# Expert weight ring of eight blocks, two of them over buffers of the first mixer, and an expert loop of four experts per turn

## The chip, the cores and the metric

One core of one Trainium2 chip runs the whole program in one launch. The metric is the device time in microseconds (us) of one execution. The kernel before takes 1587.86 us, the median of 3 runs (1586.34 to 1592.57).

## The reference, cut to what matters

Two transformer blocks follow one another on one sequence of 256 tokens with 1024 features, all in float32. The change lies in the first block, at the seam between its mixer and its routed experts:

```
def first_block(x, ...):
    mix = token_mixer(x, ...)            # x @ w_in, sliding-window attention beside
                                         # gated spatial mixing, then @ w_out
    h   = layer_norm(2**0.25 * x + mix)
    ffn = routed_experts(h, ...)         # 32 experts, 4 per token, d_ff = 1024
    return layer_norm(2**0.25 * h + ffn)

def expert(xb):                          # xb: the rows routed to this expert
    gt  = minimum(xb @ w_gate + b_gate, 7)
    up  = clip(xb @ w_up + b_up, -7, 7)
    hid = gt * sigmoid(1.702 * gt) * (up + 1)
    return hid @ w_down + b_down         # then times the token's gate, added to its row
```

Each expert has three 1024 x 1024 float32 matrices, 12 MB; all 32 experts together have some 400 MB. The second block (RWKV-7 mixing, block attention, a gated feed-forward layer with a convolution) is not touched, apart from where some of its inputs lie.

## The kernel before, in words

**Memory.** There are two areas in SBUF. `ring` has 24576 floats per partition, `work` has 27500. During the experts `ring` is six slots of 4096 floats (`SLOTS = 6`, `SLOT = 4096`, 2 MB per block over 128 partitions). An expert is six blocks: blocks 0 to 3 hold two 128-row slices each of gate and up weights (`UP_SLOTS = 4`), blocks 4 and 5 hold four slices each of the down weights. Block j of every expert goes to slot j. Before the experts, `ring` holds `w_in` (slots 0 to 3) and `w_out` (slots 4 and 5) of the mixer. `work` holds everything else: constants, the broadcast bias and norm rows (`rows_sb`), the attention and gating tensors, x (`x_nat`), h.

**The order of the loads.** All large loads are issued by SyncE (SP) on one queue, in program order. For the first expert (L448 to L451) it waits until the projections are done (`proj_done` 6), issues slots 0 to 3, waits until the whole mixer product is done (`mix_done` 4), and issues slots 4 and 5. It then waits for `iter_ready` (the routing is known), issues seven small loads for the second block (L454 to L462), reads two loop counts, and enters its loop. A turn of the loop (L465 to L469) is one expert: for each of the six slots it waits until TensorE has used the slot's old block and issues the new one. After the loop it issues the weights of the second block in half buffers (L471 to L477); the first four halves go into the area of slots 0 and 1 and wait for the last expert to be through with these slots.

**The expert loop on the engines.** The number of turns is 32 as long as no expert has more than 64 rows. In one turn TensorE (PE) adds the biases (L669), multiplies the four up blocks (L692), gathers the rows of the next expert (L652), scatters the result of the expert before (L661), transposes (L705, L709), multiplies the two down blocks (L719). ScalarE and VectorE do the activation and the copies between these. Each matmul group waits for its slot by a count that rises by 16 per turn (`slot_in[j]`), and adds one to `slots_used`, by which SP refills. Every instruction of the turn stands once in the program and is run 32 times.

**Around it.** Before the loop PE does the mixer's output product (`project_out`, L603) in two halves: slices 0 to 3 of `w_out` for both token tiles, then slices 4 to 7. Then come the layer norm on VectorE, the router product (L631) and the counts (L640 to L644). GpSimd (POOL) computes the low-order parts of h (L2022, L2024, semaphore `rest_ready`).

Of the kernel before, what the change touches and what calls it, by code (L numbers as in the profile page):

```python
# [33 lines left out]
SLOTS = 6  # L34
UP_SLOTS = 4
SPLITS = 3
BIAS_ROWS = SPLITS * NE
# [6 lines left out]

ROWS = [("b_in_vug", W_VUG), ("ln_v_g", G1), ("ln_v_b", G1), ("b_router", NE), ("sinks", NQ),
        ("b_out", D), ("ln1_g", D), ("ln1_b", D), ("ln2_g", D), ("ln2_b", D)]
COLUMNS = [("b_in_qk", 5), ("b_s", NG)]
# [64 lines left out]
def program(nc, A, out):  # L112
    ctx = ExitStack()
    with ctx:
        def sem(name):
            return ctx.enter_context(nc.semaphore(name))
# [23 lines left out]
        cols_sb = take(cols_n)  # L140
        rows_sb = take(rows_n)
        const = lambda n: const_sb[:, const_at[n][0]:sum(const_at[n])]
# [10 lines left out]
        def little(*shape):  # L153
# [13 lines left out]
        ss1, rms1 = little(TT), little(TT)  # L167
        w_router = take(KD * NE).rearrange("p (k e) -> p k e", k=KD)
        n_iter = ctx.enter_context(nc.sbuf_tensor("n_iter", [1, 2], I32))

# [3 lines left out]
        w_out = ring[:, 16384:24576].rearrange("p (k n) -> p k n", k=KD)  # L174
        x_nat = take(TT * D).rearrange("p (t d) -> p t d", t=TT)
# [8 lines left out]
        prob = take(3 * 1024)  # L184
        prob0 = prob[:, 0:1024].rearrange("p (h s) -> p h s", h=NQ)
# [20 lines left out]
        place = pool2[:, 2560:2624].bitcast(BF16).rearrange("p (t s) -> p t s", t=TT)  # L206
        alpha_ident = take(P)
        bias_area = take(3 * D // 2)
        bias_parts = bias_area.bitcast(BF16)
# [15 lines left out]
            sem(n) for n in ("pT_done", "pT_ready", "attn_done", "attn_ready", "sguT_done", "sguT_ready"))  # L225
        mix_done, var_ready, std_ready, h_ready, hT_done, hT_ready = (
            sem(n) for n in ("mix_done", "var_ready", "std_ready", "h_ready", "hT_done", "hT_ready"))
# [3 lines left out]
        slot_in = [sem(f"slot_in{i}") for i in range(SLOTS)]  # L231
        slots_used = sem("slots_used")
# [183 lines left out]

        def slot_area(j):
            return ring[:, j * SLOT:(j + 1) * SLOT]

        def up_slot(j):  # L420

            return slot_area(j).rearrange("p (b k n) -> p b k n", b=2, k=2)

        def down_slot(j):
            return slot_area(UP_SLOTS + j).rearrange("p (k n) -> p k n", k=4)

        @block.sync
        def _(sp):
# [4 lines left out]
            sp.dma_start(cols_sb, A["columns"]).then_inc(consts_in, 16)  # L433
            mix_n = rows_at["b_out"][0]
            sp.dma_start(rows_sb[:, 0:mix_n], A["rows"][0:mix_n].partition_broadcast(P)).then_inc(consts_in, 16)

# [5 lines left out]
            sp.dma_start(x_nat, A["x"].rearrange("(t p) d -> p t d", p=P)).then_inc(ln_rows_in, 16)  # L442
            sp.dma_start(rows_sb[:, mix_n:rows_n], A["rows"][mix_n:rows_n].partition_broadcast(P)).then_inc(ln_rows_in, 16)
# [18 lines left out]
            sp.dma_start(rows2_sb, A["rows2"].partition_broadcast(P)).then_inc(small2_in, 16)  # L462
            n = sp.value_load(n_iter[0:1, 0:1], min_val=NE, max_val=NE * PASSES)
            n_rest = sp.value_load(n_iter[0:1, 1:2], min_val=NE - 1, max_val=NE * PASSES - 1)
            with sp.Fori(1, n) as it:  # L465
                e = it % NE
                for j in range(SLOTS):
                    sp.wait_ge(slots_used, sp.snap(it * SLOTS - (SLOTS - j - 1)))
                    sp.dma_start(slot_area(j), expert_slot(e, j)).then_inc(slot_in[j], 16)  # L469

            for n2, (f, half) in enumerate(HALVES):  # L471
                if n2 < 4:
                    sp.wait_ge(slots_used, sp.snap(n_rest * SLOTS + n2 * HBUF // SLOT + 1))
                else:
                    sp.wait_ge(half_used, n2 - 3)
                w = half_width(f)
                sp.dma_start(half_view(n2), A[f"w2_{f}"][:, half * w:(half + 1) * w]).then_inc(half_in[n2 % 4], 16)  # L477
# [35 lines left out]
        def _(pe):  # L513
# [86 lines left out]
            def project_out(t, ks):  # L600
                for n in range(2):
                    for k in ks:
                        ins = pe.matmul(bank[mix_bank[t][n]][:, :], mixT[:, k, t * P:(t + 1) * P], w_out[:, k, n * BANK:(n + 1) * BANK],  # L603
                                        start=k == 0, stop=k == KD - 1)
                    if ks[-1] == KD - 1:
                        ins.then_inc(mix_done, 1)

            pe.wait_ge(attn_ready, 2)
# [68 lines left out]
            pe.wait_ge(iter_ready, 1)  # L677
            n = pe.value_load(n_iter[0:1, 0:1], min_val=NE, max_val=NE * PASSES)
            with pe.Fori(0, n) as it:
                now, ahead, landed = pe.snap(it + 1), pe.snap(it + 2), pe.snap(it * 16 + 16)  # L680

# [31 lines left out]
                for j in range(SLOTS - UP_SLOTS):  # L713
                    pe.wait_ge(slot_in[UP_SLOTS + j], landed)
                    w = down_slot(j)
# [6 lines left out]
            pe.wait_ge(y_ready, pe.snap(n + 1))  # L722
            pe.wait_ge(place_T_ready, pe.snap(n + 1))
            scatter(True).then_inc(acc_done, 1)
# [420 lines left out]
        def _(act):  # L1145
# [61 lines left out]
            act.wait_ge(iter_ready, 1)  # L1207
            n = act.value_load(n_iter[0:1, 0:1], min_val=NE, max_val=NE * PASSES)
            with act.Fori(0, n) as it:
                now, ahead = act.snap(it + 1), act.snap(it + 2)  # L1210
                act.wait_ge(gt_ready, now)
# [4 lines left out]
                act.copy(hidT, bank[4][:, :].rearrange("p (j c) -> p j c", j=4)).then_inc(hidT_ready, 1)  # L1216
                act.wait_ge(slots_used, act.snap(it * SLOTS + SLOTS))
                act.copy(yy, bank[7][:, :]).then_inc(y_ready, 1)  # L1218

            for n2 in range(2):  # L1220
# [227 lines left out]
        def _(dve):  # L1448
# [177 lines left out]
            link(dve.tensor_reduce(n_iter_f[0:1, 0:1], bank[4][0:1, 0:NE], AX.X, ALU.max))  # L1626
            link(dve.tensor_scalar(passes, const("thresholds")[0:1, :], n_iter_f[0:1, 0:1], float(NE), ALU.is_lt, ALU.mult))
            link(dve.tensor_reduce(n_iter_f[0:1, 1:2], passes, AX.X, ALU.add))
# [19 lines left out]
            build_place(1)  # L1648
            n = dve.value_load(n_iter[0:1, 0:1], min_val=NE, max_val=NE * PASSES)
            with dve.Fori(0, n) as it:  # L1650
                now = dve.snap(it + 1)
                dve.wait_ge(slots_used, dve.snap(it * SLOTS + UP_SLOTS))
                dve.tensor_scalar(gt, bank[4][:, :], LIMIT, None, ALU.min).then_inc(gt_ready, 1)  # L1653
# [7 lines left out]
                dve.wait_ge(place_T_done, now)  # L1661
                pick(bass.ds((it + 1) % NE, 1))
                dve.tensor_copy(place_T, bank[5][:, 0:T]).then_inc(place_T_ready, 1)
                build_place(it + 2)
                build_place_g(it + 1)

# [442 lines left out]
```

## Time and profile before

| | |
|---|---|
| median of 3 runs | 1587.86 us (1586.34 to 1592.57) |
| the profiled execution | 1587.55 us, its span 1585.7 us |
| mean granted TensorE clock | 0.984 |
| PE busy | 1454.2 us (92%) |
| DMA, HBM read | 489.73 MB, mean 309 GB/s over the span |
| chain of waits: share of DMA of expert weights | 45% |
| chain of waits: share of PE | 46% |

The span is what lies between the first and the last instruction. The execution's own time is 1.85 us longer than its span. The page's strip of 40 slices has slices of 39.6 us: one digit is the busy share in tenths. The chain of waits follows the work that ended last back in time, so its shares tell which resource set the end, while busy shares do not.

### The profile page before, as it was taken

The page shows a single profiled execution, that of the slowest core. Times are in us where ns is not written, and L with a number is a line of the kernel's source. Part 1 is how long each engine was busy: PE and PEld are TensorE (multiplying, and loading weights), DVE is VectorE, ACT ScalarE, POOL GpSimd, SP SyncE. Part 2 cuts the span into 40 slices and gives each one's busy share as a digit, 9 for nine tenths or more (in the row PEclk, how much of TensorE's full clock was granted, in tenths as well). Part 3 has the DMA queues.
Part 4 walks back from the last instruction along what each step waited for, and adds up shares of the span by engine and source line. Part 5 has one row for each costly group of instructions (what it writes and reads, how often), then busy time and mean ns, then how long its engine had stood idle before and what let it go on. Part 6 is the DMA issues. An engine that isn't in the chain of part 4 may idle for free.

```text
span 1585.7 us, 22051 instructions
## 1 busy us (share of the span) xinstructions
PE 1454.2 (92%) x9246; PEld 806.3 (51%) x9246; DVE 515.2 (32%) x888; ACT 365.5 (23%) x507; POOL 70.7 (4%) x34
## 2 busy tenths in 40 slices
PE   8989998989989989989889889869998999999998
PEld 6543333323333333333333333339777895489997
DVE  1762211112112112111111111156794535266565
ACT  0531111101101101101111111135545220244542
POOL 0020000000000000000000000000000000023322
PEclk9999999999999999999999999989999989999999
DMA  9659999999999999999999999945440015135552
GB/s 366 222 227 367 429 428 429 428 428 429 428 428 428 429 429 429 429 427 429 429 429 428 428 428 429 429 187 171 148 139 21 2 54 235 45 136 185 188 193 80
DMA packets 44527, 491.24 MB, mean 310 GB/s; under 512 B 4944, under 2 KB 5456, under 8 KB 13168
## 3 DMA queue, kind: packets, MB, share of 16 engines
q1 hardware_dynamic: 44352, 490.66, 75.2%
q8 instruction: 24, 0.39, 0.1%
q10 hardware_dynamic: 144, 0.13, 0.0%
q14 instruction: 7, 0.06, 0.0%
HBM read 489.73 MB, written 1.05 MB: 309 GB/s over the span
## 4 chain that ended last, share of the span: by engine, by line
PE 46%; DMA 45%; DVE 5%; ACT 3%; issue 1%; SPq 0%; DVEq 0%; ACTq 0%
DMA ring<-in_w_exp 45%; PE bank L692 10%; PE bank L740 5%; PE bank L741 5%; PE bank L742 5%; PE bank L719 2%; PE bank L1065 2%; PE bank L603 2%; PE bank L1103 2%; PE bank L521 1%; PE bank L551 1%; DVE ring_parts L1684 1%; PE bank L661 1%; PE bank L652 1%; PE bank L908 0%
## 5 line engine op out<-in xcount | busy, mean ns | idle before, releaser
L692 PE MATMUL bank<-ring,work 128*64 128x512 f32 x2048 | 460.8, 596 | 67.8 <-DMA ring<-in_w_exp 67.8
L692 PEld LDWEIGHTS bank<-ring,work 128*64 128x64 f32 x2048 | 139.4, 136 | 371.4 <-issue 227.9
L1653 DVE TENSOR_SCALAR work<-bank 128x512 f32<-128x512 f32 x32 | 22.1, 692 | 721.9 <-PE bank L692 721.9
L719 PE MATMUL bank<-ring,work 128*64 128x512 f32 x1024 | 226.8, 595 | 14.6 <-ACT work L1216 14.6
L719 PEld LDWEIGHTS bank<-ring,work 128*64 128x64 f32 x1024 | 70.6, 137 | 150.2 <-issue 128.0
L740 PE MATMUL bank<-work_parts,ring_parts 128*128 128x256 f32 x472 | 132.8, 281 | 5.4 <-DVE work_parts L1702 5.4
L1212 ACT ACTIVATE work<-work 128x512 f32<-128x512 f32 x32 | 20.2, 631 | 500.3 <-DVE work L1653 500.3
L741 PE MATMUL bank<-work_parts,ring_parts 128*128 128x256 f32 x472 | 133.2, 282 | 0.0
L742 PE MATMUL bank<-work_parts,ring_parts 128*128 128x256 f32 x472 | 133.0, 282 | 0.0
L740 PEld LDWEIGHTS bank<-work_parts,ring_parts 128*128 128x128 f32 x472 | 91.1, 193 | 6.4 <-issue 5.7
L741 PEld LDWEIGHTS bank<-work_parts,ring_parts 128*128 128x128 f32 x472 | 90.6, 192 | 0.8
L742 PEld LDWEIGHTS bank<-work_parts,ring_parts 128*128 128x128 f32 x472 | 90.7, 192 | 0.0
L740 PE MATMUL bank<-ring_parts,work_parts 128*128 128x512 f32 x200 | 80.5, 402 | 3.2 <-DVE ring_parts L1684 2.5
L741 PE MATMUL bank<-ring_parts,work_parts 128*128 128x512 f32 x200 | 79.2, 396 | 0.0
L742 PE MATMUL bank<-ring_parts,work_parts 128*128 128x512 f32 x200 | 79.0, 395 | 0.0
L1401 ACT CAST ring_parts<-ring 128x2048 fp32r<-128x2048 f32 (+1 forms) x44 | 63.4, 1467 | 50.2 <-PE bank L742 50.2
L1218 ACT COPY work<-bank 128x512 f32<-128x512 f32 x32 | 18.8, 586 | 230.0 <-PE bank L719 230.0
L661 PE MATMUL bank<-work 64*128 64x512 f32 x264 | 65.6, 614 | 0.7 <-ACT work L1218 0.7
L2036 POOL TENSOR_TENSOR ring_parts<-ring,ring_parts 128x1024 fp32r<-128x1024 f32 x22 | 55.9, 2541 | 225.5 <-ACT ring_parts L1401 225.5
L652 PEld LDWEIGHTS bank<-work 128*128 128x128 bf16 x1584 | 49.9, 98 | 26.9 <-issue 26.9
L1980 DVE TENSOR_TENSOR ring_parts<-ring,ring_parts 128x2048 fp32r<-128x2048 f32 x21 | 54.1, 2575 | 21.0 <-ACT ring_parts L1401 21.0
L2030 POOL TENSOR_TENSOR ring<-ring,work 128x512 f32<-128x512 f32 x4 | 5.1, 1276 | 1168.1 <-DVE ring L1878 1168.1
(392 smaller groups left out, 1609.3 us busy)
## 6 DMA issues: line engine op xcount, KB each, us to landing
ring<-in_w_exp SPq DMA_DIRECT2D x192, 2048.0 KB, 24.1
ring<-in_ffn_up SPq DMA_DIRECT2D x22, 1024.0 KB, 4.8
ring<-in_ffn_down SPq DMA_DIRECT2D x22, 512.0 KB, 3.3
ring<-in_w_in SPq DMA_DIRECT2D x2, 2048.0 KB, 16.7
ring<-in_w_out SPq DMA_DIRECT2D x4, 1024.0 KB, 16.7
ring<-in_w_k SPq DMA_DIRECT2D x4, 1024.0 KB, 5.0
ring<-in_w_v SPq DMA_DIRECT2D x4, 1024.0 KB, 4.9
ring<-in_w_gate_a SPq DMA_DIRECT2D x4, 1024.0 KB, 4.9
```

The lines of the kernel that those rows point to most:

```text
L603: ins = pe.matmul(bank[mix_bank[t][n]][:, :], mixT[:, k, t * P:(t + 1) * P], w_out[:, k, n * BANK:(n + 1) * BANK], start=k == 0, stop=k == ...
L652: ins = pe.matmul(x_bank[:, k * CAP:(k + 1) * CAP], h_part[:, part, t, k * P:(k + 1) * P], place[:, t, :], start=n == 0, stop=n == 5, skip ...
L661: ins = pe.matmul(bank[2 * t + n][:, :], place_T[lo:lo + CAP, t * P:(t + 1) * P], yy[lo:lo + CAP, :], start=False, stop=stop, skip_group_c ...
L692: ins = pe.matmul(to[n2 * CAP:(n2 + 1) * CAP, :], x_e[:, 2 * j + kk, :], w[:, b, kk, n2 * BANK:(n2 + 1) * BANK], start=False, stop=j == UP ...
L719: ins = pe.matmul(y_bank[n2 * CAP:(n2 + 1) * CAP, :], hidT[:, k % 4, k // 4 * CAP:(k // 4 + 1) * CAP], w[:, kk, n2 * BANK:(n2 + 1) * BANK] ...
L740: pe.matmul(to, left[0], right[0], start=start, stop=False, skip_group_check=True)
L741: pe.matmul(to, left[0], right[1], start=False, stop=False, skip_group_check=True)
L742: return pe.matmul(to, left[1], right[0], start=False, stop=stop, skip_group_check=True)
L1065: ins = pe.matmul(bank[to[n2] + t][:, :], yT[:, k, t * P:(t + 1) * P], tail[f][:, k, n2 * BANK:(n2 + 1) * BANK], start=k == 0, stop=k == N ...
L1401: act.copy(ff_hi[i][:, cols], ff_land[i][:, cols]).then_inc(ff_upper[i], 1)
L1980: dve.tensor_tensor(ff_rest[i][:, 0:2 * D], ff_land[i][:, 0:2 * D], ff_hi[i][:, 0:2 * D].bitcast(F32), ALU.subtract).then_inc(up_rest[i], 1)
L2036: pool.tensor_tensor(ff_rest[i][:, 2 * D:FF], ff_land[i][:, 2 * D:FF], ff_hi[i][:, 2 * D:FF].bitcast(F32), ALU.subtract).then_inc(down_res ...
```

## The change: what it does

- The ring gets eight slots (`RING = 8`). Slots 6 and 7 lie in `work`. Slot 6 lies over the end of `rows_sb`, over `wsT`, `qkT` and `v_nat`; slot 7 lies over `ug` (which also holds h) and `x_nat`. For this the rows, `prob`, `x_nat`, `alpha_ident` and `bias_area` get other places; the sizes and numbers of their loads stay.
- Blocks go round the ring: block number n of the whole stream goes to slot n mod 8. As 24 blocks are four experts and three rounds, the loop's turn on every engine becomes four experts (`TURN = 4`), written out, and there are 8 turns for 32 experts.
- Before the loop SP issues eight blocks, in the order 0, 1, 2, 3, 6, 4, 5, 7. Block 6 (expert 1, block 0) waits for the gating product and the last biases. Block 4 waits for a new semaphore after the first half of the mixer's output product (`mix_first`). Block 5 waits for `mix_done` 4, as before. Block 7 waits for `rest_ready` 4 and `router_done` 2.
- SP's loop runs one turn less than the others, with 24 refills per turn (blocks 8 to 31 counted from the turn's first block); the last 16 refills stand behind it. The half buffers wait for the blocks that last lie in slots 0 and 1.

```diff
+RING = 8
+TURN = 4
+PER_TURN = TURN * SLOTS // RING
@@
+        prob = take(3 * 1024)
+        seventh_at = top[0] - 3 * 1024 - SLOT
+        eighth_at = top[0]
         ug = take(2 * TT * G1)
+        x_nat = take(TT * D).rearrange("p (t d) -> p t d", t=TT)
@@
-        def slot_area(j):
-            return ring[:, j * SLOT:(j + 1) * SLOT]
+        def slot_area(s):
+            return ring[:, s * SLOT:(s + 1) * SLOT] if s < SLOTS else work[:, (seventh_at, eighth_at)[s - SLOTS]:][:, 0:SLOT]
+        def slot_of(turn, j):
+            return (turn * SLOTS + j) % RING
+        def landed_count(it, turn, j):
+            return (it * PER_TURN + (turn * SLOTS + j) // RING + 1) * 16
@@ SP
-            for j in range(SLOTS):
-                if j == UP_SLOTS:
-                    sp.wait_ge(mix_done, 4)
-                sp.dma_start(slot_area(j), expert_slot(0, j)).then_inc(slot_in[j], 16)
+            for s in (0, 1, 2, 3, 6, 4, 5, 7):
+                if s == 6:
+                    sp.wait_ge(mixed_done, 1)
+                    sp.wait_ge(ug_biased, 4)
+                if s == 4:
+                    sp.wait_ge(mix_first, 1)
+                if s == 5:
+                    sp.wait_ge(mix_done, 4)
+                if s == 7:
+                    sp.wait_ge(rest_ready, 4)
+                    sp.wait_ge(router_done, 2)
+                sp.dma_start(slot_area(s), expert_slot(s // SLOTS, s % SLOTS)).then_inc(slot_in[s], 16)
@@ SP
-            with sp.Fori(1, n) as it:
-                e = it % NE
-                for j in range(SLOTS):
-                    sp.wait_ge(slots_used, sp.snap(it * SLOTS - (SLOTS - j - 1)))
-                    sp.dma_start(slot_area(j), expert_slot(e, j)).then_inc(slot_in[j], 16)
+            def refill(it, load):
+                s = load % RING
+                e = (it * TURN + load // SLOTS) % NE
+                sp.wait_ge(slots_used, sp.snap(it * (TURN * SLOTS) + (load - RING + 1)))
+                sp.dma_start(slot_area(s), expert_slot(e, load % SLOTS)).then_inc(slot_in[s], 16)
+            with sp.Fori(0, n_rest) as it:
+                for load in range(RING, RING + TURN * SLOTS):
+                    refill(it, load)
+            for load in range(RING, TURN * SLOTS):
+                refill(n_rest, load)
@@ half buffers
-                    sp.wait_ge(slots_used, sp.snap(n_rest * SLOTS + n2 * HBUF // SLOT + 1))
+                    sp.wait_ge(slots_used, sp.snap(n_rest * (TURN * SLOTS) + (TURN * SLOTS - RING + 1 + n2 * HBUF // SLOT)))
@@ PE
-            project_out(1, range(0, 4))
+            project_out(1, range(0, 4)).then_inc(mix_first, 1)
@@ PE, ACT and DVE alike: the body of the loop becomes expert(it, turn)
-                    pe.wait_ge(slot_in[j], landed)
-                    w = up_slot(j)
+                    s = slot_of(turn, j)
+                    pe.wait_ge(slot_in[s], pe.snap(landed_count(it, turn, j)))
+                    w = up_slot(s)
...
+            with pe.Fori(0, n) as it:
+                for turn in range(TURN):
+                    expert(it, turn)
@@ DVE
-            link(dve.tensor_scalar(passes, ..., float(NE), ALU.is_lt, ALU.mult))
+            link(dve.tensor_scalar(passes, ..., float(NE // TURN), ALU.is_lt, ALU.mult))
```

## Rows read from the trace of the kernel before

**Rows 1.** The page: the instruction queue, then the chain's shares by engine.

```profile
q8 instruction: 24, 0.39, 0.1%
...
PE 46%; DMA 45%; DVE 5%; ACT 3%; issue 1%; SPq 0%; DVEq 0%; ACTq 0%
```

**Rows 2.** The chain that ended last: start us, length us, what.

```profile
149.51 13.73 PE bank L692 x64
...
175.82 13.73 PE bank L692 x64
...
216.04 23.44 DMA ring<-in_w_exp
...
243.35 25.50 DMA ring<-in_w_exp
...
272.72 25.50 DMA ring<-in_w_exp
```

**Rows 3.** Stretches: busy us (count) per engine, clock, DMA share, GB/s.

```profile
43.00:49.00 6.00, 6.00 (x25) 3.32 (x24) 4.65 (x7) 5.20 (x23) 0.00 (x0) 1.00 0.96 410
...
93.00:101.00 8.00, 8.00 (x22) 3.61 (x21) 5.84 (x9) 0.29 (x1) 0.00 (x0) 1.00 0.00 1
...
113.00:120.00 7.00, 4.31 (x28) 2.07 (x27) 5.85 (x23) 3.00 (x6) 2.84 (x2) 0.74 0.00 0
122.00:127.00 5.00, 5.00 (x25) 1.74 (x26) 2.34 (x10) 1.87 (x2) 0.00 (x0) 0.88 0.79 252
...
400.00:1000.00 600.00, 540.04 (x3338) 197.14 (x3334) 80.67 (x200) 75.30 (x102) 0.00 (x0) 1.00 1.01 428
```

**Rows 4.** Timeline of SP: its first small load and its first refill.

```profile
120.16 0.33 SPq L454 DMA_DIRECT2D work<-in_consts  x1
...
127.16 0.36 SPq L469 DMA_DIRECT2D ring<-in_w_exp  x1
```

**Rows 5.** Timelines of POOL and PE: what ends rest_ready and router_done 2.

```profile
114.86 2.14 POOL L2024 TENSOR_TENSOR work<-work 128x1024 bf16<-128x1024 f32 x1 [1.16 <-ACT work L1188]
...
118.07 0.39 PE L642 MATMUL bank<-work 128*128 128x32 f32 x2
```

**Rows 6.** Blocks 0 to 3 (L451), few issues per window: issue, landing.

```profile
L451 SPq DMA_DIRECT2D ring<-in_w_exp x1: 347/347/347, 69.2 to 69.2; - x1
...
DMA to landing us min/median/max: 7.6/7.6/7.6
...
L451 SPq DMA_DIRECT2D ring<-in_w_exp x2: 432/432/432, 69.6 to 70.0; - x2
...
DMA to landing us min/median/max: 12.1/14.3/16.5
...
L451 SPq DMA_DIRECT2D ring<-in_w_exp x1: 534/534/534, 70.5 to 70.5; - x1
...
DMA to landing us min/median/max: 22.5/22.5/22.5
```

**Rows 7.** DMA queues, 86 to 93 us: packets, MB, share of 16 engines.

```profile
q8 instruction: 1, 0.02, 1.0%
```

**Rows 8.** The same, 139 to 150 us, then 150 to 1060 us (no q8).

```profile
q8 instruction: 1, 0.02, 0.5%
...
q1 hardware_dynamic: 26751, 384.79, 99.4%
```

**Rows 9.** L469: landing of the refill issued at 127.2, and the one at 137.1.

```profile
DMA to landing us min/median/max: 9.5/9.5/9.5
...
L469 SPq DMA_DIRECT2D ring<-in_w_exp x1: 333/333/333, 137.1 to 137.1; - x1
...
DMA to landing us min/median/max: 14.3/14.3/14.3
```

**Rows 10.** Second block, 1073 to 1089 us, and the queues of 1073 to 1090.

```profile
1073.00:1089.00 16.00, 16.00 (x139) 16.00 (x139) 11.21 (x20) 7.61 (x8) 0.00 (x0) 1.00 0.58 198
...
q8 instruction: 2, 0.03, 0.8%
```

More of the change, by code:

```diff
@@ L43 @@
 W_QK, W_QKV, W_VUG = 640, 768, 1152
-ROWS = [("b_in_vug", W_VUG), ("ln_v_g", G1), ("ln_v_b", G1), ("b_router", NE), ("sinks", NQ),
-        ("b_out", D), ("ln1_g", D), ("ln1_b", D), ("ln2_g", D), ("ln2_b", D)]
+ROWS = [("b_out", D), ("ln1_g", D), ("ln1_b", D), ("ln2_g", D), ("ln2_b", D),
+        ("b_router", NE), ("sinks", NQ), ("b_in_vug", W_VUG), ("ln_v_g", G1), ("ln_v_b", G1)]
 COLUMNS = [("b_in_qk", 5), ("b_s", NG)]
@@ L140, in program @@
         cols_sb = take(cols_n)
-        rows_sb = take(rows_n)
         const = lambda n: const_sb[:, const_at[n][0]:sum(const_at[n])]
@@ L168, in program @@
         w_router = take(KD * NE).rearrange("p (k e) -> p k e", k=KD)
+        alpha_ident = take(P)
+        bias_area = take(3 * D // 2)
+        rows_sb = take(rows_n)
         n_iter = ctx.enter_context(nc.sbuf_tensor("n_iter", [1, 2], I32))
@@ L174, in program @@
         w_out = ring[:, 16384:24576].rearrange("p (k n) -> p k n", k=KD)
-        x_nat = take(TT * D).rearrange("p (t d) -> p t d", t=TT)
         r2_at = top[0]
@@ L225, in program @@
             sem(n) for n in ("pT_done", "pT_ready", "attn_done", "attn_ready", "sguT_done", "sguT_ready"))
-        mix_done, var_ready, std_ready, h_ready, hT_done, hT_ready = (
-            sem(n) for n in ("mix_done", "var_ready", "std_ready", "h_ready", "hT_done", "hT_ready"))
+        mix_first, mix_done, var_ready, std_ready, h_ready, hT_done, hT_ready = (
+            sem(n) for n in ("mix_first", "mix_done", "var_ready", "std_ready", "h_ready", "hT_done", "hT_ready"))
         router_done, top_ready, top_exp, chosen_ready = (
@@ L230, in program @@
         iter_ready, split_ready = sem("iter_ready"), sem("split_ready")
-        slot_in = [sem(f"slot_in{i}") for i in range(SLOTS)]
+        slot_in = [sem(f"slot_in{i}") for i in range(RING)]
         slots_used = sem("slots_used")
@@ L415, in expert_slot, with up_slot, down_slot @@
             return A["w_exp"][bass.ds(e, 1), j, :, :].rearrange("o p n -> p (o n)")
-        def slot_area(j):
-            return ring[:, j * SLOT:(j + 1) * SLOT]
[L420 to L425, printed above, removed]
+        def slot_area(s):
[4 more added lines that the diff above has]
+            return (it * PER_TURN + (turn * SLOTS + j) // RING + 1) * 16
+        def up_slot(s):
+            return slot_area(s).rearrange("p (b k n) -> p b k n", b=2, k=2)
+        def down_slot(s):
+            return slot_area(s).rearrange("p (k n) -> p k n", k=4)
         @block.sync
@@ L433, in _ @@
             sp.dma_start(cols_sb, A["columns"]).then_inc(consts_in, 16)
-            mix_n = rows_at["b_out"][0]
-            sp.dma_start(rows_sb[:, 0:mix_n], A["rows"][0:mix_n].partition_broadcast(P)).then_inc(consts_in, 16)
+            mix_at = rows_at["b_router"][0]
+            sp.dma_start(rows_sb[:, mix_at:rows_n], A["rows"][mix_at:rows_n].partition_broadcast(P)).then_inc(consts_in, 16)
             sp.dma_start(w_in[:, :, W_QKV + G1:], A["w_in"][:, :, W_QKV + G1:]).then_inc(w_g_in, 16)
@@ L442, in _ @@
             sp.dma_start(x_nat, A["x"].rearrange("(t p) d -> p t d", p=P)).then_inc(ln_rows_in, 16)
-            sp.dma_start(rows_sb[:, mix_n:rows_n], A["rows"][mix_n:rows_n].partition_broadcast(P)).then_inc(ln_rows_in, 16)
+            sp.dma_start(rows_sb[:, 0:mix_at], A["rows"][0:mix_at].partition_broadcast(P)).then_inc(ln_rows_in, 16)
             sp.wait_ge(attn_done, 1)
@@ L606, in project_out @@
                         ins.then_inc(mix_done, 1)
+                return ins
             pe.wait_ge(attn_ready, 2)
@@ L677, in _, with expert @@
             pe.wait_ge(iter_ready, 1)
-            n = pe.value_load(n_iter[0:1, 0:1], min_val=NE, max_val=NE * PASSES)
-            with pe.Fori(0, n) as it:
-                now, ahead, landed = pe.snap(it + 1), pe.snap(it + 2), pe.snap(it * 16 + 16)
+            n = pe.value_load(n_iter[0:1, 0:1], min_val=NE // TURN, max_val=NE * PASSES // TURN)
+            def expert(it, turn):
+                now, ahead = pe.snap(it * TURN + (turn + 1)), pe.snap(it * TURN + (turn + 2))
                 pe.wait_ge(place_T_ready, now)
@@ L713, in _ @@
                 for j in range(SLOTS - UP_SLOTS):
-                    pe.wait_ge(slot_in[UP_SLOTS + j], landed)
-                    w = down_slot(j)
+                    s = slot_of(turn, UP_SLOTS + j)
+                    pe.wait_ge(slot_in[s], pe.snap(landed_count(it, turn, UP_SLOTS + j)))
+                    w = down_slot(s)
                     for kk in range(4):
@@ L1207, in _, with expert @@
             act.wait_ge(iter_ready, 1)
-            n = act.value_load(n_iter[0:1, 0:1], min_val=NE, max_val=NE * PASSES)
-            with act.Fori(0, n) as it:
-                now, ahead = act.snap(it + 1), act.snap(it + 2)
+            n = act.value_load(n_iter[0:1, 0:1], min_val=NE // TURN, max_val=NE * PASSES // TURN)
+            def expert(it, turn):
+                now, ahead = act.snap(it * TURN + (turn + 1)), act.snap(it * TURN + (turn + 2))
                 act.wait_ge(gt_ready, now)
@@ L1216, in _ @@
                 act.copy(hidT, bank[4][:, :].rearrange("p (j c) -> p j c", j=4)).then_inc(hidT_ready, 1)
-                act.wait_ge(slots_used, act.snap(it * SLOTS + SLOTS))
+                act.wait_ge(slots_used, act.snap(it * (TURN * SLOTS) + (turn + 1) * SLOTS))
                 act.copy(yy, bank[7][:, :]).then_inc(y_ready, 1)
+            with act.Fori(0, n) as it:
+                for turn in range(TURN):
+                    expert(it, turn)
             for n2 in range(2):
@@ L1648, in _, with expert @@
             build_place(1)
[L1649 to L1652, printed above, removed]
+            n = dve.value_load(n_iter[0:1, 0:1], min_val=NE // TURN, max_val=NE * PASSES // TURN)
+            def expert(it, turn):
+                now = dve.snap(it * TURN + (turn + 1))
+                dve.wait_ge(slots_used, dve.snap(it * (TURN * SLOTS) + (turn * SLOTS + UP_SLOTS)))
                 dve.tensor_scalar(gt, bank[4][:, :], LIMIT, None, ALU.min).then_inc(gt_ready, 1)
@@ L1661, in _ @@
                 dve.wait_ge(place_T_done, now)
-                pick(bass.ds((it + 1) % NE, 1))
+                pick(bass.ds((it * TURN + (turn + 1)) % NE, 1))
                 dve.tensor_copy(place_T, bank[5][:, 0:T]).then_inc(place_T_ready, 1)
-                build_place(it + 2)
-                build_place_g(it + 1)
+                build_place(it * TURN + (turn + 2))
+                build_place_g(it * TURN + (turn + 1))
+            with dve.Fori(0, n) as it:
+                for turn in range(TURN):
+                    expert(it, turn)
             def norm(t, rms):
```

12 lines of the change are left out of this document (4 added, 8 removed).

## The prediction

> **What bounds the kernel now.** I read the chain of waits first. DMA and PE share it almost evenly [rows 1], and in order of time it changes hands once in the expert loop. The first experts follow one another at PE's own pace, 175.82 - 149.51 = 26.31 us each. From 216.04 each expert ends on a transfer of weights, and the period is 272.72 - 243.35 = 29.37 us [rows 2]. The stretches say why: from 400 to 1000 us the DMA engines are fully busy at 428 GB/s [rows 3]. An expert is six blocks, so a block takes 29.37 / 6 = 4.895 us of all DMA engines. The loop is a stream of blocks at that pace. PE has 3.06 us to spare per expert. A deeper ring cannot make a saturated stream faster. It can only let the stream start earlier, in time in which the DMA engines now stand still. The stretches show such time: 93 to 101 us (share 0.00), 113 to 120 us (0.00), and some of 122 to 127 us (0.79) [rows 3].
>
> **Part 1, two blocks out of the loop.** Block 6 waits for things that are over before block 3 is in, and follows block 3 on the queue. Blocks 6 and 4 then fill 93 to 101 us. Block 5 goes out when it does now. Block 7 waits for POOL, which ends at 114.86 + 2.14 = 117.00, and for PE's L642, which ends at 118.46 [rows 5]. So it goes out near 118.5 us. The refills then have 184 blocks to bring instead of 186: -2 x 4.895 = -9.8 us.
>
> **Part 2, block 7 in front of the small loads.** The seven small loads go out from 120.16 us, as now, and the first refill at 127.16 [rows 4]. Block 7 is 118.5 to 120.16 = 1.7 us ahead of them and holds the engines for 4.9 us, so they are pushed back by 3.2 us. The idle fifth of 122 to 127 us can take up 0.21 x 5 = 1.05 us of it. So the refills begin 2.2 to 3.2 us later than now. I take the middle: +2.7 us. The small loads themselves are needed only after the loop.
>
> **Part 3, instruction fetches of PE inside the stream.** The profile has a queue q8 of kind instruction: 24 packets, 0.39 MB, so 16 KB each [rows 1]. Their size against the program points to PE. In the second block two of them lie in one dense stretch of 139 matmuls and 139 weight loads [rows 10], so a fetch brings about 260 to 280 instructions. PE runs 3338 matmuls and as many weight loads in 600 us of loop [rows 3], that is 163 of each per expert, 327 instructions. A turn of one expert is 1.2 fetches long. A turn of four is 1308 instructions and some for registers, 4.8 to 5.1 fetches. Now one fetch falls into the first turn (139 to 150 us), and none into 150 to 1060 us: the turn stays in the engine's memory [rows 8]. With four experts per turn I count four more fetches in the first turn, all in the saturated stream.
>
> What does one cost? Blocks 0, 1, 2 landed at 76.8, 81.7 and 86.5 us, 4.9 us apart. Block 3 landed at 70.5 + 22.5 = 93.0, 6.5 us behind block 2 [rows 6]. In that stretch one fetch ran [rows 7]. A block is in when the slowest of the 16 DMA engines has its share in. I read the 1.6 us as one engine held up by the fetch. A saturated stream never gives this back: the others are full too, but the landing waits for the late one. If all fetches of PE use the same engine, four of them add 4 x 1.6 = 6.4 us to it.
>
> That engine has some slack. The fetch at 139 to 150 us moved no landing: the refills of 127.2 and 137.1 landed at 136.7 and 151.4, three blocks in 14.7 us, 4.9 each [rows 9]. The first refill took 9.5 us to land against 7.6 alone [rows 6, 9], so some engine was 1.9 us behind the rest then, from uneven small loads. The fetch's engine was not that one: it had 1.9 us of room and used 1.6. With four more it ends 6.4 - 0.3 = 6.1 us behind where the slowest is now.
>
> This is the number between far ends. Below, it is 0: four fetches on four engines, each within the 1.9 us of room. Above, it is a fetch of every page in every turn (a rival below). I take 6.1, because the one fetch that hit a full stream with no slack moved a landing.
>
> **Edits at nothing.** The register arithmetic for each slot and turn on PE, ACT and DVE is hidden by PE's 3.06 us to spare per expert; it would have to exceed that to show, and costs up to some tenths in the last expert. SP waits for `slots_used` between refills and has several blocks queued. SP has no new wait in the loop; in front of it stand the waits of blocks 6 and 4, with block 5 behind them, all over before 101 us, and that of block 7, over before `iter_ready`. The half buffers stay behind the last block on the queue. Transfers into `work` run as fast as into `ring`: 43 to 49 us, with rows and x going to `work`, shows 410 GB/s at share 0.96, 427 per full share, against 428 [rows 3]. The bound from 410 would be 4% on a quarter of the blocks, 9 us; I take 0. The lead of eight blocks makes PE run at its own pace some three experts longer, and changes no end.
>
> **The sum.** -9.8 + 2.7 + 6.1 = -1.0 us. The profiled execution took 1587.55 us with a span of 1585.7, 0.31 under the median, so the difference carries over to the median: 1587.86 - 1.0 = 1586.9 us. All work behind the loop moves with its end. Changes under 0.5% (7.9 us) can't be told from none in this kernel.
>
> **Rival 1, the fetches cost nothing visible** (other engines, or a fetch that takes only its share). The sum is -9.8 + 2.7 = -7.1: 1580.8 us. For it: the fetch of 139 to 150 us moved no landing. Against it: block 3. If the idle parts also take all of block 7, it is -9.8: 1578.1 us, the most that this change can give.
>
> **Rival 2, slower: PE's turn no longer stays in its memory.** A turn of about five fetches is run eight times. If less than six pages are kept, each turn fetches them all again: 8 x 5.5 = 44 fetches instead of one, each on a full stream. That is 44 x 1.6 - 1.9 = 68.5 us more, and with parts 1 and 2 1587.86 - 7.1 + 68.5 = 1649 us. PE's own stall at each jump back hides in its 4 x 3.06 us per turn; the price is in the late DMA engine. For it: nothing here has a turn longer than 1.3 fetches. Against it: no fetch was made again when the turn crossed a page at each pass [rows 8]. It decides from the number of pages kept.
> The Trainium skill states this rule, in "Runtime: NRT & Kernel Launch", section "Instruction fetch mechanics": a taken branch to a target outside the current two-page window forces a fetch of the target page. By it the time is that of rival 2. The same section gives PE room for 128 KiB, by which the turn fits and nothing is fetched twice. The trace sides against a window of two: the fetch of the page ahead did not push out the loop's first page.
>
> **Rival 3, the blocks in `work` are slower, or the added instructions delay the end:** up to +9 us on -1.0, 1596 us. Only the 410 speaks for it.
>
> **How the numbers follow.** My forecast 0.45, rival 1 0.28 (of which 0.05 near the full 9.8), rival 2 0.17, rival 3 0.10. The range reaches from the full gain (1578.5) to somewhat short of rival 3 (1594) and leaves out rival 2 and a little at each end. Faster by over 0.5% needs under 1579.9: the best part of rival 1 and a share of its spread, 0.14. Slower by over 0.5% needs over 1595.8: rival 2 and half of rival 3, 0.22. The rest, 0.64, is no change that can be told.
>
> **What would show it.** Right: stretches 93 to 101 and 118 to 124 us busy on DMA; the first transfer that ends an expert two to three experts later than 216 us; a period of still 29.37 us at the end; q8 with some four more packets, all before 250 us; single landings of the first turn 6.5 us behind the one before instead of 4.9. Rival 1: the same q8 count and landings 4.9 us apart throughout, the loop's end 7 us earlier. Rival 2: q8 with over 60 packets, a mean period over 31 us. I am wrong altogether if the period changes without more fetches, or if the part behind the loop changes its length by more than 1 us.

## The result and the profile after

The changed kernel takes 1577.55 us (median of 5 runs, 1576.71 to 1578.58) against 1587.87 us (5 runs of before, 1586.34 to 1596.17). The ratio is 0.9922, with a 95% interval of 0.9895 to 0.9949. Its profiled execution took 1577.55 us with a span of 1575.6. A second set of runs, shown below, gave 1578.7 us and 0.9934 (0.9912 to 0.9955). The forecast was 1586.9 us, within 1578.5 to 1594.0: the time lies under the range, and the kernel is faster by 9 to 10 us where 1 us was forecast.

The page after. The columns are those of [rows 1] and [rows 3].

```profile
span 1575.6 us, 21819 instructions
...
DMA  9579999999999999999999999945440015145552
...
q8 instruction: 28, 0.46, 0.1%
...
PE 61%; DMA 29%; DVE 5%; ACT 3%; issue 1%; SPq 0%; DVEq 0%; ACTq 0%
```

q8 has four more packets than in [rows 1]. The DMA share of the chain fell from 45% to 29% without the stream getting any faster. In the full stream the chain now has one piece of DMA per two experts, 35.30 of 58.74 us, where it had 25.50 of each 29.37 us [rows 2]. Both chains belong to a stream of the same pace, so the shares of the chain say little on how much one resource bounds.

The chain in order of time (start us, length us, what):

```profile
150.78 13.74 PE bank L725 x64
...
177.10 13.74 PE bank L725 x64
...
256.11 13.74 PE bank L725 x64
...
289.47 30.77 DMA ring<-in_w_exp
...
343.70 35.28 DMA ring<-in_w_exp
...
402.45 35.30 DMA ring<-in_w_exp
...
461.19 35.30 DMA ring<-in_w_exp
...
1025.11 3.65 PE bank L725 x16
```

PE's own pace is the same (26.32 us per expert). The first transfer in the chain starts at 289 us, where it was 216 us in [rows 2]. From then on two experts take 461.19 - 402.45 = 58.74 us, 29.37 each, as before. The last line is PE's work on the last up block of the last expert, for which it waited at the end of the stream. Before, the same group starts 7.3 us later:

```profile
1032.40 3.65 PE bank L692 x16
```

The stretches after (busy us and counts, clock, DMA share, GB/s):

```profile
93.00:101.00 8.00, 8.00 (x20) 3.50 (x19) 5.84 (x9) 0.29 (x1) 0.00 (x0) 1.00 0.94 398
103.00:111.00 8.00, 4.84 (x28) 3.33 (x29) 7.74 (x9) 3.62 (x7) 5.20 (x2) 0.96 0.57 233
113.00:118.00 5.00, 4.75 (x12) 2.58 (x11) 3.10 (x10) 2.33 (x2) 3.17 (x2) 0.58 0.00 0
...
122.00:127.00 5.00, 5.00 (x46) 2.58 (x45) 3.47 (x14) 1.87 (x2) 0.00 (x0) 0.80 0.90 381
400.00:1000.00 600.00, 538.38 (x3346) 197.34 (x3343) 81.22 (x201) 54.15 (x85) 0.00 (x0) 1.00 1.01 429
```

The idle time of [rows 3] between 93 and 101 us is filled by blocks 6 and 4. The stretch from 122 to 127 us went from 0.79 to 0.90. 113 to 118 us is still empty. The stream itself has the same 429 GB/s.

SP's timeline, to be read against [rows 4]: block 7 goes out 1.62 us ahead of the small loads. The fence behind it is the summary of the DMA of the first refill, which takes 9.6 us to land.

```profile
119.80 0.33 SPq L473 DMA_DIRECT2D work<-in_w_exp  x1
121.42 0.33 SPq L476 DMA_DIRECT2D work<-in_consts  x1
...
126.26 1.20 SPq L484 DMA_DIRECT2D work<-in_rows  x1
```

```profile
DMA to landing us min/median/max: 9.6/9.6/9.6
```

q8 by stretch, the answer to [rows 8]: one fetch from 139 to 150 us, and four from 150 to 1060 us, where there were none.

```profile
q8 instruction: 1, 0.02, 0.6%
...
q1 hardware_dynamic: 26546, 381.73, 98.6%
q8 instruction: 4, 0.07, 0.0%
```

The difference between the two first profiles splits into two parts. The start of the last x16 group moved by 1032.40 - 1025.11 = 7.3 us. From that group to the end of the span there are 1585.7 - 1032.40 = 553.3 us before and 1575.6 - 1025.11 = 550.5 after, 2.8 us less. Together 10.1. The first part is the size of rival 1 (7.1 us). The second was in no forecast. The experiments ask for both.

### The profile page after: what moved, and what is told of

Read it like the earlier page. It is cut to its first block, busy times and chain, and to the rows that moved or that the text cites. A ratio compares the mean times of both kernels' runs of the same rounds, so it can differ in the third digit from the quotient of the medians.

```text
span 1575.6 us, 21819 instructions
## 1 busy us (share of the span) xinstructions
PE 1450.7 (92%) x9246; PEld 807.8 (51%) x9246; DVE 514.4 (33%) x888; ACT 334.5 (21%) x483; POOL 70.6 (4%) x34
## 4 chain that ended last, share of the span: by engine, by line
PE 61%; DMA 29%; DVE 5%; ACT 3%; issue 1%; SPq 0%; DVEq 0%; ACTq 0%
DMA ring<-in_w_exp 29%; PE bank L725 14%; PE bank L753 9%; PE bank L778 5%; PE bank L779 5%; PE bank L780 5%; PE bank L691 2%; PE bank L682 2%; PE bank L1103 2%; PE bank L632 2%; PE bank L1141 2%; PE bank L550 1%; PE bank L699 1%; PE bank L580 1%; PE bank L738 1%; ACT work L1256 1%
## 5 line engine op out<-in xcount | busy, mean ns | idle before, releaser
L725 PE MATMUL bank<-ring,work 128*64 128x512 f32 x1536 | 344.2, 596 | 45.8 <-DMA ring<-in_w_exp 45.8
L725 PEld LDWEIGHTS bank<-ring,work 128*64 128x64 f32 x1536 | 105.8, 136 | 270.5 <-issue 173.7
L753 PE MATMUL bank<-ring,work 128*64 128x512 f32 x768 | 170.1, 595 | 11.6 <-ACT work L1256 11.6
L725 PE MATMUL bank<-work 128*64 128x512 f32 x512 | 115.1, 595 | 14.9 <-DMA work<-in_w_exp 14.9
L753 PEld LDWEIGHTS bank<-ring,work 128*64 128x64 f32 x768 | 53.5, 137 | 112.7 <-issue 101.6
L725 PEld LDWEIGHTS bank<-work 128*64 128x64 f32 x512 | 34.9, 135 | 90.2 <-issue 58.6
L1258 ACT COPY work<-bank 128x512 f32<-128x512 f32 x32 | 18.7, 586 | 230.6 <-PE bank L753 230.6
```

What stands on the lines that cost most here:

```text
L725: ins = pe.matmul(to[n2 * CAP:(n2 + 1) * CAP, :], x_e[:, 2 * j + kk, :], w[:, b, kk, n2 * BANK:(n2 + 1) * BANK], start=False, stop=j == UP ...
```

## The experiments

Every profile is split at the same place, the start of the last x16 group of up matmuls. "Stream end" is that start; "behind" is the span less it. The first refill's landing is taken from the completions in the trace. A ratio goes by runs of before taken beside the experiment; their medians are 1587.78, 1587.53 and 1588.34 us in the three sets of experiments.

| kernel | total us (median, runs) | span | first refill landed | stream end | behind |
|---|---|---|---|---|---|
| before | 1587.87 (5) | 1585.7 | 136.7 | 1032.40 | 553.3 |
| before, second profile | 1588.60 (1) | 1586.8 | 136.1 | 1033.02 | 553.8 |
| before, third profile | 1586.03 (1) | 1584.2 | 136.6 | 1032.36 | 551.8 |
| changed | 1577.55 (5) | 1575.6 | 138.4 | 1025.11 | 550.5 |
| changed, second | 1578.70 (6) | 1576.5 | 137.4 | 1024.84 | 551.7 |
| changed, third | 1578.46 (1) | 1576.5 | 136.7 | 1023.67 | 552.8 |
| ring 6, turn 4 | 1587.44 (10) | 1586.4 | 137.8 | 1033.55 | 552.9 |
| ring 8, turn 8 | 1587.05 (10) | 1584.6 | 136.6 | 1031.07 | 553.5 |
| changed, small loads late | 1577.75 (5) | 1575.9 | 136.0 | 1023.17 | 552.7 |
| before, small loads late | 1586.15 (10) | 1584.6 | 134.4 | 1031.43 | 553.2 |
| block 7 behind small loads | 1581.79 (8) | 1581.2 | 141.5 | 1028.39 | 552.8 |
| small loads early | 1577.39 (6) | 1574.9 | 134.7 | 1021.93 | 553.0 |

### The long turn alone

```diff
-RING = 8
+RING = 6
-            for s in (0, 1, 2, 3, 6, 4, 5, 7):
+            for s in (0, 1, 2, 3, 4, 5):
```

> The changed kernel with RING = 6 and TURN = 4: no blocks beyond six, blocks 4 and 5 wait as in the changed kernel, the loop is four experts long. It isolates the long turn. Theory A (my forecast's step: all instruction fetches of PE fall on one DMA engine and add 1.6 us each to it): the last up block of expert 31 lands 6 us later than in the kernel before (1032.4), near 1038.5, total near 1594. Theory B (each fetch delays another of the 16 engines, only the largest delay counts): last up block near 1033, total 1588 to 1589. Both: q8 has 28 packets. Theory C (the part behind the loop changes its length with the granted clock, not with the edits): from the last up block to the end lies between 550.4 us (as in the changed kernel) and 553.3 us (as before), whatever the ring.

Measured: 1587.44 us, ratio to before 0.9992 (0.998 to 1.0004). Its page, then its chain:

```profile
q8 instruction: 28, 0.46, 0.1%
```

```profile
1033.55 3.65 PE bank L725 x16
```

q8 has 28 packets, as expected. The stream end is at 1033.55, 1.15 us later than in the first profile of before, and the first refill landed 1.1 us later as well. From first refill to stream end it takes 895.8 us, as in before (895.7). Four experts per turn and their four more fetches cost nothing here. The completions show why: 15 of the 16 parts of the first refill landed 2.3 us or more ahead of the slowest one, and the fetches moved only such parts. Theory A, on which my forecast stood, wanted 6 us more and falls. The run has no block 7, and yet its first refill landed later than that of before. What made it late is not shown, and it bears on part 2 of the forecast (below).

### A turn of eight

```diff
-TURN = 4
+TURN = 8
```

> The changed kernel with TURN = 8: a turn of some 2700 PE instructions, ten to eleven pages of 16 KB, run 4 times. It asks whether PE's pages are fetched again when the turn is longer than what is kept. If eight pages or fewer are kept: q8 grows by 30 to 45 packets against 28, all in the stream. Then theory A (one engine): 40 x 1.5 = 60 us later, near 1637; theory B (spread over 16): 40 x 1.5 / 16 = 3.8 us on each engine, some 4 to 7 us on the worst, 1581 to 1585. If all pages of the turn are kept: q8 near 34, and total 1577 to 1579.

Measured: 1587.05 us, 0.999 (0.9977 to 1.0004). The whole gain is gone. Its page, then its queues from 150 to 1060 us:

```profile
q8 instruction: 69, 1.13, 0.3%
```

```profile
q1 hardware_dynamic: 26491, 380.99, 98.5%
q8 instruction: 45, 0.74, 0.3%
```

That is 41 fetches more than in the changed kernel, so a turn of eight experts is fetched again at each pass, and one of four is not. The chain shows where the price falls (start us, length us, what):

```profile
1031.07 3.65 PE bank L725 x16
```

First refill to stream end is 894.5 us, against 886.7, 887.4 and 887.0 in the three profiles of the changed kernel: 7.4 us for 41 fetches, 0.18 us each. On one DMA engine it would have been some 61 us. Theory B expected 4 to 7 us at the stream and a total of 1581 to 1585. The stream came out a little above that, the total by 2 us. The range was counted from the first profile of the changed kernel, which is the shortest of all behind the loop.

The single completions of each block explain the 0.18. The trace has 16 completion times per block but doesn't name the DMA engine of each, so a part is told here by its distance to the slowest one. Between fetches these distances stay the same to some 0.2 us. The list is worked out from the trace of the changed kernel:

```
fetch at   part moved, us against the slowest (from -> to)   slowest moved
143.0      -1.1 -> becomes the slowest                       +0.5
164.9      -1.6 -> -0.1                                      0.0
183.1      -1.2 -> becomes the slowest                       +0.3
203.3      -2.1 -> -0.6                                      0.0
223.8      -2.2 -> -0.8                                      0.0
```

Each fetch holds up one DMA engine by 1.5 us, near the 1.6 that I read from block 3. But it is another engine each time. Landing follows the slowest only, and with five fetches the distances of up to 2.2 us swallow most of it. In the second profile of the changed kernel one fetch hit an engine without room and moved the slowest by 1.55 us.

In the turn of eight there are too many fetches for such room. Its completions show the pattern. The list has, for each fetch in order, how far the part that it moved lay from the slowest one before:

```
fetches from 577.8 us:  -0.91 -0.64 -1.39 -1.67 -2.35 -2.71 -2.17 -2.17
fetches from 753.1 us:  -0.94 -0.74 -1.39 -1.67 -2.36 -2.74 -2.16 -2.15
fetches from 901.4 us:  -0.94 -0.73 -1.42 -1.68 -2.38 -2.78
```

The distances come back after eight fetches: PE's fetches go round eight of the 16 DMA engines. The end of the stream says the same. Counted from the slowest part of the first refill, at 4.895 us per block, eight parts of the last up block lie between -1.7 and +0.3 us, and the other eight between +6.4 and +8.6. So a round of eight fetches moves the slowest by 1.5 us, and 41 fetches by 41 x 1.5 / 8 = 7.7 us, an estimate beside the 7.4 measured. Theory B was right that the fetches are spread, but over 8 engines and not 16, which is why its 3.8 us for each was too low.

### The small loads behind the stream

```diff
             sp.wait_ge(iter_ready, 1)
-            ... the seven small loads
...
             for n2, (f, half) in enumerate(HALVES):
+                if n2 == 2:
+                    ... the seven small loads
```

> The changed kernel with the seven small loads moved from ahead of the loop to behind the last expert block (between the second and the third half buffer). Part 2 of the forecast (small loads push the refills back): the first refill lands near 136.3 instead of 138.4, the last up block near 1023.0 instead of 1025.1, total 2 to 3 us less than the changed kernel, 1575. Rival: the small loads are then late for the second block (first wanted near 1056): total the same or up to 5 us more. Nothing else moves.

Measured: 1577.75 us, 0.9932 (0.9915 to 0.9948). The first refill landed at 136.0 and the stream ended at 1023.17, 1.9 us before that of the first changed profile, as expected, and 1.4 before the mean of the three. The total didn't follow: the median lies between the two of the changed kernel (1577.55 and 1578.70). The part behind was 552.7 us, within the changed kernel's own 550.5 to 552.8, so no run shows the rival of late small loads. A fetch moved the slowest completion by 1.3 us right after the start, where the engines are closer together.

The same edit was made in the kernel before, with its ring of six and turn of one:

> The kernel before (six blocks, turn of one) with the same move of the small loads. Part 2's mechanism alone: first refill lands at 127.2 + 7.6 = 134.8 or earlier instead of 136.7, so 1.9 to 2.5 us less than the kernel before, 1585.5. Rival as in the other kernel: late small loads eat it.

Measured: 1586.15 us, 0.9985 (0.9972 to 0.9998), a gain of 1.6 us. The first refill landed at 134.4, 2.3 us earlier than in the first profile of before. The stream ended at 1031.43, 1.0 us earlier. So the first refill lands 1.5 to 2.1 us earlier without the small loads ahead of it, against the mean of either kernel's three profiles. Half of it came through to the end here: the fetch at 140.8 us moved the slowest completion by 1.0 us. The rival (late loads eat it) did not show.

### The same two kernels again

No edit: the changed kernel and the kernel before, profiled a second time.

> The changed kernel once more, unchanged, for a second profile and more timed rounds. In its first profile the last up block landed 7.3 us earlier than before, and what lies behind the loop was 2.8 us shorter, with less time at the low granted clock (27.0 us behind the loop against 33 to 34 us in five other profiles). Theory C (that shorter part is the clock's state in that run): a second profile can have 525 to 526.5 us behind the first transposes of the second block, and the median of the total drifts towards 1587.8 - 7.3 = 1580.5. Theory D (the edits shorten the second block, for instance by other places of its buffers): 523.5 us again and a median near 1577.5.

Measured: 1578.7 us. Stream end 1024.84, behind 551.7, 1.2 us more than in the first profile, as theory C has it. The median lies between those of the two theories.

> The kernel before once more, unchanged, for a second profile of its parts. Theory C: the part behind the loop can be anything from 523 to 527 us. Theory D: 526 us again. The last up block lands within 1 us of 1032.4 by both; a larger difference would mean that single profiles can't tell one or two us apart in the loop.

Measured: 1588.6 us, one run. Stream end 1033.02, within the 1 us that was expected, behind 553.8.

### Block 7 behind the small loads

```diff
-            for s in (0, 1, 2, 3, 6, 4, 5, 7):
+            for s in (0, 1, 2, 3, 6, 4, 5):
...
             sp.dma_start(rows2_sb, A["rows2"].partition_broadcast(P)).then_inc(small2_in, 16)
+            sp.wait_ge(rest_ready, 4)
+            sp.dma_start(slot_area(7), expert_slot(1, 1)).then_inc(slot_in[7], 16)
```

> The changed kernel with block 7 issued behind the seven small loads instead of ahead of them, still ahead of the loop. It asks what block 7's place costs or brings. DMA stands still between 109 and 120 us in either case, so the engines have the same work from 120 us on, 1 to 2 us less of it hidden: the last up block lands 0 to 2 us later than in the changed kernel (1025.1 to 1027), total up to 2 us more. If the push of the small loads (part 2) were a loss of its own, it would be faster instead.

Measured: 1581.79 us, 0.9957 (0.994 to 0.9973). Its chain:

```profile
1028.39 3.65 PE bank L724 x16
```

The stream ended 3.3 us later than in the first profile of the changed kernel, and 3.9 later than the mean of its three. I expected 0 to 2. Block 7 now goes out at 125.46 us and lands at 136.6, where the first refill landed in the kernel before. It takes a place in the full stream, and only block 6 is still a gift. The stream end gains 4.0 us on before here, near the 4.9 of one block, and 7.3 with block 7 in front. So block 7's early place is worth 3.3 to 3.9 us of its 4.9. The rest, 1.0 to 1.6 us, is of the size of part 2, but no run separates what it is made of.

### Small loads in the empty time

```diff
                 if s == 7:
+                    sp.wait_ge(router_done, 1)
+                    ... the small loads of const2, cols2, w_lora_up, pos, rows2
                     sp.wait_ge(rest_ready, 4)
```

> The changed kernel with five of the seven small loads (all but the two of w_gate_up) issued as soon as the router has read hT, whose area they fill, near 114.7 us, so they run in time in which DMA stands still; block 7 and the refills are not pushed back. Part 2's mechanism: first refill near 136.3 instead of 137.4 to 138.4, last up block near 1023.0 (changed kernel 1025.1 and 1024.8), as with the small loads behind the loop, and the total 1.5 to 2.5 us under the changed kernel, 1576. Rival: the smaller unevenness of the 16 engines leaves less room for the four fetches, which then give back up to 1.5 us.

Measured: 1577.39 us, 0.9921 (0.9896 to 0.9945). Its stretch from 113 to 120 us:

```profile
113.00:120.00 7.00, 4.43 (x24) 1.98 (x23) 5.85 (x23) 3.00 (x6) 2.96 (x2) 0.74 0.78 250
```

DMA is busy where it stood still. The first refill landed at 134.7, and the stream ended at 1021.93, the earliest of all, 2.6 us before the mean of the changed kernel's three. The rival has a share in it: fetches moved the slowest completion by 1.3 us in sum. The median is 0.2 to 1.3 us under the two of the changed kernel, which these runs can't tell from none. One of its six runs took 1565.99 us, 10.8 us less than the next, at a mean granted clock of 0.991 against 0.983 to 0.985. It has no profile, and its cause is open.

### Third profiles

No edit here either: a third profile of each.

> The changed kernel unchanged, a third profile. If what lies behind the loop is shorter by chance of the clock's state (theory C), it can be 525.5 to 527 us here; if the edits shorten it (theory D), 523.5 to 524.7 again. Last up block 1024.5 to 1025.5 by both.

> The kernel before unchanged, a third profile. Theory C: the part behind the loop may fall under 525.5; theory D: 526 to 527 again. Last up block 1032 to 1033 by both.

Measured: the changed kernel's part behind was 552.8 us, before's 551.8. The order is turned round. The stretch in question has the same work in every profile: the start of a dense PE group in the second block, some 131 us behind the last x16 group, ahead of which PE has waited some 2.5 us for VectorE. The first two fences are the first profiles, before's and the changed kernel's, the others their third profiles (the number just before the DMA share is the granted clock; 1.00 is the full 2.4 GHz):

```profile
1164.00:1168.00 4.00, 4.00 (x12) 3.09 (x12) 3.96 (x3) 0.10 (x1) 0.00 (x0) 0.57 0.29 121
...
1218.00:1226.00 8.00, 5.89 (x28) 5.52 (x29) 0.00 (x0) 2.84 (x6) 0.00 (x0) 0.57 0.00 0
```

```profile
1157.00:1161.00 4.00, 4.00 (x19) 3.23 (x18) 3.97 (x3) 0.00 (x0) 0.00 (x0) 1.00 0.30 125
1211.00:1219.00 8.00, 6.84 (x52) 6.60 (x51) 0.00 (x0) 1.41 (x3) 0.00 (x0) 0.79 0.00 0
```

```profile
1164.00:1168.00 4.00, 3.49 (x15) 2.90 (x16) 3.96 (x3) 1.14 (x1) 0.00 (x0) 1.00 0.51 209
1218.00:1226.00 8.00, 6.40 (x45) 6.20 (x46) 0.00 (x0) 2.34 (x5) 0.00 (x0) 0.79 0.00 0
```

```profile
1155.50:1159.50 4.00, 4.00 (x12) 3.13 (x12) 3.96 (x3) 0.24 (x2) 0.00 (x0) 0.57 0.21 88
1209.50:1217.50 8.00, 6.02 (x30) 5.64 (x32) 0.00 (x0) 2.72 (x6) 0.00 (x0) 0.57 0.00 0
```

The third fence is before's third profile, the fourth the changed kernel's. With the clock at 0.57 (most of the stretch at the lower level, 1.2 GHz) PE starts 12 matmuls in four microseconds, with 1.00 15 to 19. In the second profiles the same stretch has 0.59 in before and 1.00 in the changed kernel. Either kernel can have either. By this stretch the six profiles fall into two groups: with the low clock the part behind is 553.3, 553.8 (before) and 552.8 us (changed), without it 551.8 (before), 551.7 and 550.5 (changed). It is not the whole account: before with the small loads late has 1.00 there and 553.2 us. Theory C holds as far as these profiles go: the means behind are 553.0 and 551.7 us, 1.3 apart, with 2.0 and 2.3 us of spread within one kernel. That none of this 1.3 is due to the edits is not shown.

## Why the prediction was wrong, point by point

- **What bounds.** Right. The stream's pace stayed at 29.37 us per expert, and the gain came from starting it earlier in time that was idle.
- **Part 1, two blocks, -9.8 us.** Right. The period and the number of blocks bear the 9.8 out. Block 6 alone gave 4.0 us at the stream's end, both with their side costs 7.3 in the first profiles, and 8.1 between the means of three profiles (1032.59 to 1024.54).
- **Part 2, the pushed small loads, +2.7 us.** Too large: the first refill landed 1.0 us later on average (136.5 to 137.5). Small loads ahead of the first refill delay it in all but one profile: counted from the end of L642 (L672 in the changed kernel), it landed after 18.2, 16.2 and 18.4 us in before's profiles and after 18.6, 19.3 and 18.7 in the changed kernel's, and after 16.1 to 16.2 in the three runs with all or most of the small loads elsewhere. That block 7 adds to this is not shown. The ring of six with a turn of four has no block 7, and took 19.3 us. Block 7 went out at 119.80 in the first profile, not 118.5, but at 118.22 and 118.08 in the others: the end of the routing itself moves by more than 1 us between runs of one program.
- **Part 3, the fetches, +6.1 us.** This is the step that failed: "If all fetches of PE use the same engine, four of them add 4 x 1.6 = 6.4 us to it." The four fetches came, in the first turn, and the delay of one DMA engine is 1.5 us, near the 1.6 forecast. But PE's fetches go round eight engines, each falls on another one, and the slowest of the 16 moved by 0.8, 1.6 and 1.1 us in the three profiles. Fetches cost before something too (1.1 us in its second profile, none in the others). The net of the step is +0.8 us, the difference of the means (1.2 - 0.4). I had weighed one event with no slack (block 3) against one with slack, and both fitted either theory. The size came from a hypothesis that no row bore out, joined with a rule on rings from the Trainium skill ("DMA: Bandwidth & Descriptors", "Queues, rings and completion order"). That rule says that a row and an engine make a ring; it does not say that a sequencer's fetches stay in one ring. The turn of eight decides it: 0.18 us per fetch where one engine would give 1.5 and eight give 1.5 / 8 = 0.19.
- **Sum for the stream.** -9.8 + 1.0 + 0.8 = -8.0 us, against 8.1 less between the means. The last two terms are read from the same completions, so this is an account of the 8.1 and no second proof of it.
- **Behind the loop, forecast as unchanged to 1 us.** Wrong as a bound for one profile: before varies from 551.8 to 553.8 us, the changed kernel from 550.5 to 552.8. So the 2.8 us of the first pair, which by the prediction's own sign would have made it wrong altogether, overstate what the edits do here. How much of the 1.3 between the means is theirs stays open.
- **Rival 1** was the right one: 7.1 us for the stream. Its time of 1580.8 us was missed by the 1.7 us too much in part 2, less the 0.8 of the fetches, and by what lies behind the loop. Its sign of landings 4.9 us apart throughout did not hold: one step was 6.45 us in the second profile of the changed kernel, and the longest of the others 5.4. But single landings 1.6 us late, the sign for my forecast, are no sign of one shared engine either: before's second profile has a step of 5.97 at its one fetch.
- **Rival 2** named a true mechanism at the wrong length. The turn of four stays; the turn of eight is fetched again. The Trainium skill's "Runtime: NRT & Kernel Launch", section "Instruction fetch mechanics", states both a window of two pages and 128 KiB for PE. The runs agree with the second: a turn of about 1300 instructions, some 84 KB at 64 bytes each (an estimate from 256 instructions per 16 KiB on that page), is not fetched again, and one of twice that is. Its price was far too high, though, for the same reason as part 3: 44 fetches were to cost 68.5 us, and 41 took 7.4.
- **Rival 3** did not show: 429 GB/s with a quarter of the blocks in `work`, and the ring of six with the same added instructions took the time of before.

The idle time that is left is 113 to 118 us. Putting the small loads there ended the stream 2.6 us earlier still and brought no gain that the medians can tell.

## What to carry to other kernels

Where a saturated stream of transfers bounds a loop, a deeper ring is worth the idle DMA time ahead of the loop, block by block, less what the rest of the change puts in the stream's way (two blocks gave 8.1 of 9.8 us here); the steady pace does not change. Price a hold-up of one DMA engine by how far the slowest of the sixteen moves, not by its own length; where many of them go round several engines, divide their sum by the number of these (here 41 fetches cost an eighth of it). Split every profile at the same instruction, and take more than one profile of each kernel before a difference of 2 us behind that point is put down to an edit.

## What the runs showed of the hardware that was not expected

- An instruction fetch of PE (16 KB) holds up one DMA engine by 1.5 us in a full stream, and successive fetches go round eight of the 16 engines: 41 more fetches made the slowest 7.4 us later, and at the end eight parts of a block lagged by 6.4 to 8.6 us while the other eight had kept their place.
- PE's turn of some 1300 instructions is fetched once (28 packets on q8 in all), one of some 2600 at each of its four passes (69 packets).
- In a saturated stream the 16 parts of a block keep their distances to some 0.2 us between fetches, for the whole 900 us. The spread at the end is 1.8 to 3.7 us in the six profiles of the two kernels. A lead or a lag once gained is not made up.
- The low stretches of the granted clock behind the loop lie at other places in different runs of the same program, and the part behind differs by 2.0 and 2.3 us in 552 between runs of one program.
